# Gate and up projections of a SwiGLU by Strassen's scheme, with the down projection as a phase of its own

## What is computed

```
def rms_norm(x, g):
    y = xf * lax.rsqrt(jnp.mean(xf * xf, axis=-1, keepdims=True) + EPS)
    return (y * g.astype(jnp.float32)).astype(x.dtype)
def swiglu(h, w_gate, w_up, w_down):
    return (jax.nn.silu(h @ w_gate) * (h @ w_up)) @ w_down

x = x + 0.5 * swiglu(rms_norm(x, ff1_norm), ff1_w_gate, ff1_w_up, ff1_w_down)   # 1024 -> 2816 -> 1024
x = x + mixer(rms_norm(x, mix_norm))
x = x + 0.5 * swiglu(rms_norm(x, ff2_norm), ff2_w_gate, ff2_w_up, ff2_w_down)
return rms_norm(x, final_norm)
```

## Time and profile before

| | us |
|---|---|
| three runs | 1892.01, 1892.21, 1893.86 |
| median | 1892.21 |
| span of the profiled execution | 1891.5 |
| TensorE busy in it | 1820.5 |
| VectorE, ScalarE, GpSimd busy | 761.9, 455.6, 431.8 |

### The profile page before, as it was taken

The page is one execution under the profiler, slowest core; times in us unless marked ns, Lnnn a source line. Parts: engine busy times, 40 slices in busy tenths (PEclk is TensorE's granted clock), DMA queues, the critical chain, the costliest instruction groups (busy, mean ns, idle before and its releaser), DMA issues.

```text
span 1891.5 us, 22799 instructions
## 1 busy us (share of the span) xinstructions
PE 1820.5 (96%) x8284; PEld 1493.1 (79%) x8284; DVE 761.9 (40%) x1067; ACT 455.6 (24%) x745; POOL 431.8 (23%) x894
## 2 busy tenths in 40 slices
PE   6899999999999999999798799999999999999998
PEld 5788888888888887788576687888888888888886
DVE  5243243334323434612864545334324333432345
ACT  6211211111111113423447434111121111111113
POOL 2588776750000002400333333000000000000003
PEclk8999999999999999899888899999999999999999
DMA  5311212121121111123922031111111111112102
GB/s 129 85 45 45 78 59 74 55 77 45 33 67 44 44 44 45 62 78 76 120 67 67 12 112 56 56 45 55 33 55 55 44 44 55 44 35 65 44 33 89
DMA packets 166442, 112.33 MB, mean 59 GB/s; under 512 B 32576, under 2 KB 156096, under 8 KB 166144
## 3 DMA queue, kind: packets, MB, share of 16 engines
q1 hardware_dynamic: 165120, 107.35, 20.8%
q0 software_dynamic: 1280, 4.42, 0.6%
HBM read 98.68 MB, written 13.07 MB: 59 GB/s over the span
## 4 chain that ended last, share of the span: by engine, by line
PE 88%; ACT 3%; SPq 3%; DVE 2%; DMA 2%; POOL 1%; issue 1%; DVEq 0%; ACTq 0%; POOLq 0%
PE bank L646 28%; PE bank L647 28%; PE bank L648 28%; POOL ssq L1689 1%; SPq L543 1%; PE bank L882 1%; PE bank L883 1%; DMA Mt<-k_scratch 1%; ACT sco L1234 0%; PE bank L884 0%; DVE htmp L1366 0%; ACT hT_hi L1056 0%; PE bank L841 0%; PE bank L661 0%; SPq L535 0%
## 5 line engine op out<-in xcount | busy, mean ns | idle before, releaser
L646 PE MATMUL bank<-hT_hi,w_lo 128*128 128x512 f32 x1728 | 685.3, 397 | 17.4 <-DVE hT_lo L1379 6.2
L647 PE MATMUL bank<-hT_lo,w_hi 128*128 128x512 f32 x1728 | 679.2, 393 | 0.0
L648 PE MATMUL bank<-hT_hi,w_hi 128*128 128x512 f32 x1728 | 678.9, 393 | 0.0
L646 PEld LDWEIGHTS bank<-hT_hi,w_lo 128*128 128x128 f32 x1728 | 328.7, 190 | 92.1 <-issue 14.7
L1332 DVE TENSOR_TENSOR w_lo<-raw,w_hi 128x1024 fp32r<-128x1024 f32 x157 | 193.0, 1240 | 480.8 <-ACT w_hi L1026 480.8
L647 PEld LDWEIGHTS bank<-hT_lo,w_hi 128*128 128x128 f32 x1728 | 328.9, 190 | 69.9 <-issue 1.9
L648 PEld LDWEIGHTS bank<-hT_hi,w_hi 128*128 128x128 f32 x1728 | 328.4, 190 | 69.4
L1689 POOL TENSOR_TENSOR ssq<-ssq,sqt 128x512 f32<-128x512 f32 x54 | 78.1, 1447 | 1106.5 <-ACT sqt L1040 1102.6
L1416 DVE SCALAR_TENSOR_TENSOR xT<-bank,xT 128x512 f32<-128x512 f32 x352 | 241.0, 690 | 188.0 <-PE bank L648 187.9
L646 PE MATMUL bank<-aT_hi,w_lo 128*128 128x512 f32 x704 | 275.1, 391 | 4.0 <-DVE aT_lo L1409 3.1
L648 PE MATMUL bank<-aT_hi,w_hi 128*128 128x512 f32 x704 | 273.9, 389 | 0.0
(11 more groups left out here) (168 smaller groups left out, 980.2 us busy)
## 6 DMA issues: line engine op xcount, KB each, us to landing
raw<-in_ff_w_gate_dram SPq DMA_DIRECT2D x44, 512.0 KB, 3.7
raw<-in_ff_w_up_dram SPq DMA_DIRECT2D x44, 512.0 KB, 3.7
raw<-in_ff_w_down_dram SPq DMA_DIRECT2D x44, 512.0 KB, 3.3
x_in<-in_x_dram SPq DMA_DIRECT2D x8, 512.0 KB, 6.2
out_dram<-osb SPq DMA_DIRECT2D x8, 512.0 KB, 2.7
raw<-in_w_out_dram SPq DMA_DIRECT2D x26, 128.0 KB, 2.9
raw<-in_w_out_dram SPq DMA_DIRECT2D x13, 256.0 KB, 3.3
raw<-in_w_in_dram SPq DMA_DIRECT2D x6, 512.0 KB, 4.2
```

The lines of the kernel that those rows point to most:

```text
L646: nc.tensor.matmul(o, wl, rh, start=first, stop=False)
L647: nc.tensor.matmul(o, wh, rl, start=False, stop=False)
L648: return nc.tensor.matmul(o, wh, rh, start=False, stop=last)
```

## The change

Gate and up matrices are now cut as 2 x 2 blocks: a pair of column tiles (f = 0, 1) by two halves of the 1024 inputs (kh = 0, 1, four k-tiles each); the activations as kh by token half h. One instance (a pair of column tiles of one matrix, 22 per block) used to be 2 x 2 x 2 = 8 block products of 12 matmuls and is now 7, in the Winograd form of Strassen's scheme: products 0 to 6 accumulate into three banks in the order c, d, c, d, c, b, c (`STEP_BANK`), and between them ACT copies the bank out (`take_snap`), because the next product adds on top. DVE forms the four weight sums of each instance (`weight_sum`), the three sums of results (`gate_c12`, `gate_c22`, `gate_c11`) and the products of gate and up (`up`). The seven activation blocks are made once per feed-forward block (`blocks`): 16 sums over 128 x 512 tiles in place, 24 rounded tiles and 24 rests beside those of product 0 (`block_hi` on ACT; `block_lo` on DVE for odd, `blocks_lo` on POOL for even tiles).

```
+STEP_BANK = "cdcdcbc"
+STEP_FIRST = (0, 1, 5)
+SNAPS = [(0, "c"), (1, "d"), (2, "c"), (4, "c")]
+        def product(n, s):
+            o = bank[inst_bank(n, STEP_BANK[s])]
+            pe.wait_ge(ws_lo_done, N_STEP * n + s + 1)
...
+            elif s == 2:
+                pe.wait_ge(snap_taken, 4 * n + SNAP_C11 + 1)
...
+            for k in range(4):
+                last = mm3(o[:, :], wk(ws_hi[s], k), wk(ws_lo[s], k), b_hi[:, k, :], b_lo[:, k, :],
+                           k == 0 and s in STEP_FIRST, k == 3, True)
```

```
+            sp.wait_ge(product_done, N_STEP * (N_INST * w + N_INST - 1) + (2, 4)[w])
+            sp.wait_ge(x_stored, 32 * (w + 1))
+            for k in range(KD):
+                sp.dma_start(xTs[w + 1][:, k, :], xs_d[:, k, :]).then_inc(x_back[k], 16)
+            store_a(w, N_PAIR - 1)
+            for t in range(2, 2 * N_PAIR):
+                load_down(w, t)
+                load_a(w, t)
```

```
-FIRST = [("G", 0, 0), ("G", 1, 0), ("U", 0, 0), ("G", 0, 1), ("G", 1, 1), ("U", 0, 1), ("U", 1, 0), ("U", 1, 1)]
+        def start(s):
+            if s == 0:
                 x_tiles(1)
                 pe.wait_ge(xt_act, 8)
                 pe.wait_ge(xt_dve, 8)
+                pe.wait_ge(normed_done, KD)
                 norm_spread(N_FF1, 1)
+        instance(0, start)
+        for n in range(1, N_INST):
+            if n == 6:
                 c_tiles()
+            instance(n)
+        for g in range(N_PAIR - 1):
+            down(0, g)
+        down(0, N_PAIR - 1, first_half(N_MIX))
```

On ACT, `blocks` puts the first snapshots between the blocks, and the first of them also waits for block 4's rests, because the snapshots lie where that block was formed:

```
+            for s in (1, 2, 4):
+                for kk in range(4):
+                    block_hi(w, s, kk)
+            take_snap(n, SNAP_C11)
+            for kk in range(4):
+                block_hi(w, 3, kk)
+            take_snap(n, SNAP_D)
...
+            if j == 0:
+                wait_hb(act, w, 4, 3)
```

More of the change, by code:

```diff
@@ new lines, in instance, with down @@
+        def instance(n, between=lambda s: None):
+            for s in range(N_STEP):
+                product(n, s)
+                between(s)
+        def down(w, g, after=lambda n: None):
+            t, i = 2 * g, g % 2
+            pe.wait_ge(w_lo_done, U_DOWN[w] + t + 2)
+            pe.wait_ge(a_lo_done, 2 * N_PAIR * w + t + 2)
+            for n in range(16):
+                d, h = n % KD, n // KD
+                c = 16 * (N_PAIR * w + g) + n
+                if n >= 3 or g:
+                    pe.wait_ge(down_taken, c - 2)
+                elif n == 0:
+                    pe.wait_ge(c11_done, N_INST * (w + 1))
+                for f in range(2):
+                    last = mm3(bank[DOWN_BANK[c % 3]][:, :], wk(wd_hi[i][:, f, :], d), wk(wd_lo[i][:, f, :], d),
+                               aT_hi[w][i][:, f, hs(h)], aT_lo[w][i][:, f, hs(h)], f == 0, f == 1)
+                last.then_inc(down_out, 1)
+                after(n)
@@ L1009, in finish, with between @@
                 out_tile((n - 11) // 2)
-        ffn(1, N_FF2, second_half(N_FF2), finish)
+        def between(s):
+            if s == 0:
+                norm_sum(N_FF2, 1)
+                norm_spread(N_FF2, 1)
+        instance(N_INST, between)
+        for n in range(N_INST + 1, 2 * N_INST):
+            instance(n)
+        for g in range(N_PAIR - 1):
+            down(1, g)
+        down(1, N_PAIR - 1, finish)
         out_tile(3)
@@ new lines, in silu @@
+        def silu(n, f, h):
+            w, j = divmod(n, N_INST)
+            dst = sg[w][:, f, hs(h)]
+            src = dst
+            if (f, h) == (1, 0):
+                act.wait_ge(product_done, N_STEP * (n + 1))
+                src = bank[inst_bank(n, "c")][:, :]
+                if j:
+                    act.wait_ge(a_done, 4 * (N_PAIR * w + j // 2))
+            else:
+                act.wait_ge({(0, 1): c12_done, (1, 1): c22_done, (0, 0): c11_done}[f, h], n + 1)
+            act.activation(dst, src, ACT.Silu).then_inc(silu_done, 1)
@@ new lines, in instance, with ahead @@
+        def instance(n, first=False):
+            w, j = divmod(n, N_INST)
+            gate = n % 2 == 0
+            def ahead(s):
+                if j < N_INST - 1:
+                    weight_hi(n + 1, s)
+                elif s in (4, 6):
+                    down_hi(w, (s - 4) // 2)
+            if not first:
+                take_snap(n, SNAP_C11)
+            ahead(0)
+            if not first:
+                take_snap(n, SNAP_D)
+            ahead(1)
+            if not first:
+                take_snap(n, SNAP_C12)
+            ahead(2)
+            ahead(3)
+            if gate:
+                silu(n, 0, 1)
+            take_snap(n, SNAP_C22)
+            ahead(4)
+            if gate:
+                silu(n, 1, 1)
+            ahead(5)
+            if gate:
+                silu(n, 0, 0)
+                silu(n, 1, 0)
+            ahead(6)
@@ L1113, in x_squares, with ffn @@
+        def ffn(w):
+            for n in range(N_INST * w + 1, N_INST * (w + 1)):
+                if n == 6:
+                    c_out()
+                instance(n)
+            for t in range(2, 2 * N_PAIR):
+                down_hi(w, t)
         def x_squares(h):
@@ L1985, in _ @@
                 take_lo(*at_, tile0=4 * (at_[0] - N_ATT), permuted=at_[0] == N_SSM)
-        norm(N_FF2)
+        for i in range(12):
+            add_square(N_FF2, i)
+        for i in range(12, 16):
+            add_square(N_FF2, i)
+            if i == 13 or i == 15:
+                blocks_lo_tile(1, 0, i - 13)
+        blocks_lo(1, 1, N_STEP)
         norm(N_END)
```

1001 lines of the change are left out of this document (641 added, 360 removed).

## The result

| | us |
|---|---|
| changed kernel, four runs | 1859.03, 1862.43, 1863.04, 1865.02, median 1862.74 |
| kernel before, four runs beside it | median 1893.03 |
| ratio | 0.9838, 95% interval 0.9824 to 0.9852 |
| span of the profiled execution | 1863.3 |

The account below looks back on a forecast made before the run. TensorE was taken to bound the kernel. The terms -119.7 + 30.3 + 38.2 + 10.6 + 3.5 = -37.1 on the span of 1891.5 gave 1854.4, forecast 1855 us; likeliest case 1835 to 1875, 8 in 10 range 1828 to 1888.

Parts of the forecast that it names:

- matmuls removed: All 44 instances: one block product of 12 matmuls fewer each, 528 x 0.2267 = -119.7 us, on TensorE at full clock.
- first start: Start of the first block: instance 0 ends at about 88.5, overhead 70.8 against 40.5, +30.3 us; bounds +18 and +40.
- second start: Start of the second block: the same stretch follows the mixer, overhead 42.5 against 4.3, +38.2 us; bounds +25 and +48.
- two seams: Between products and down, twice: 3.3 us for VectorE's product and rests, 2.0 for low clock, +10.6 us; bounds 6 and 16.
- x comes back: Reload of x, second block: loads for the second down group queue behind it and a store, +3.5 us; bounds 0 and 12.
- the turns of VectorE and GpSimd: Block starts: instructions of both engines run one after the other; without this the first stretch would end some 10 us sooner.
- the first copy behind block 4's rests: First start: ScalarE takes the first snapshot only after the rests of block 4, at 65.7 us; product 2 starts there.
- the last copy behind roundings, table load and Silu: First start: product 6 needs the last snapshot, behind four weight roundings, a table load and a Silu, done at 84.7 us.
- The products in steady state: Instances after the starts: VectorE and ScalarE fit within 19.0 us, some 1.4 us in hand per copy, 0 added.
- No cost: the small loads on GpSimd: Parameter loads moved to GpSimd's queue: from about 78 us, there by 125, needed near 150, so 0 us.
- The rival that was nearest: Parameters come too late: VectorE stops in instance 4, then ScalarE, then TensorE; 1892 us at 37 us late; chance 0.08.
- Snapshots become the bound: ScalarE between products of every instance: gain used up from 2.93 us per hand-over, 1905 us at 3.0; chance 0.12.

Follow-up runs that it names:

- run 8: Changed kernel with product 3 of each instance at 24 matmuls instead of 12, so an instance has 96 again: 1970.73 us, ratio 1.0405.
- run 1: Changed kernel with GpSimd issuing the small parameter loads right behind its two rests of block 0, only the loads of c at the end: 1856.58 us, ratio 0.9801.
- run 2: Changed kernel with the small parameter loads back on SyncE's queue, behind the stores of x and before the third weight load: 1852.07 us, ratio 0.9773.
- run 5: Changed kernel with all rests of activation blocks 1 to 6 made by VectorE, none by GpSimd: 1854.17 us, ratio 0.9791.
- runs 6 and 7: Changed kernel with each snapshot copied two and three times in every instance but the first of a block: 1863.5 and 1864.09 us, ratios 0.9842 and 0.984.
- run 3: Changed kernel with ScalarE taking the last snapshot of each block's first instance right behind its last rounding of block 6: 1838.04 us, ratio 0.9701.
- Run 4: Changed kernel with VectorE making the second pair of rests for the first down group ahead of its last two products: 1866.74 us, ratio 0.9851.
- Run 12: Changed kernel with each snapshot copied four times in every instance but the first of a block: 1897.19 us, ratio 1.0019.
- runs 3 and 11: Run 3 has its own line; run 11: changed kernel with edits of run 2, run 3, Run 4, run 5, ScalarE issuing second down group's loads: 1835.75 us, 0.9704.

## Why the prediction came out as it did

| us | forecast | measured | by |
|---|---|---|---|
| matmuls removed | -119.7 | -119.7 | spacing of 0.2267; run 8 |
| first start | +30.3 | +31.5 | instance 0 ends at 89.7, not 88.5 |
| late weight load in instance 2 | 0 | +11.3 | 8.1 and clock; runs 1 and 2 |
| second start | +38.2 | +39.1 | instance 22 ends at 1200.0: 1200.0 - 1137.6 - 19.0 = 43.4, less 4.3 |
| two seams | +10.6 | +13.3 | waits of 4.87, 3.50 and 0.53, and 1.6 and 2.8 by the low clock |
| x comes back | +3.5 | 0 | no such wait |
| not forecast | | -3.7 | see below |
| sum | -37.1 | -28.2 (spans) | |

**Right.** The starts, which are most of the cost, by their own steps: the turns of VectorE and GpSimd (run 5; the stretch took 35.6 in place of 34.3, with a wait of 1.8 us of VectorE for ScalarE in it that I had not; GpSimd's twelve instructions lasted 1.3 to 1.7 us each, and each lengthened the stretch by less than it lasted), the first copy behind block 4's rests, the last copy behind roundings, table load and Silu. The Trainium skill, "GPSIMD Engine Reference", section 1 (Specifications), says that GpSimd's SBUF interfaces are shared with VectorE, with contention when a VectorE instruction has two inputs in SBUF. The trace agrees: block 4's four sums, two inputs each, took 4.63 us beside GpSimd and 2.50 in run 5 without it. The products in steady state add nothing (runs 6 and 7).

**Wrong: "No cost: the small loads on GpSimd".** I asked when they would be there, and they were, at 122.8 (forecast 125), and VectorE's parameter work found them. What I left out is what they do to others: a 1 MB load beside them takes 32.5 us instead of 5.3. The forecast put this overlap at nothing; it cost 11.3 us. The rival that was nearest had the right transfers and the wrong victim: it let VectorE stop at the parameters, in instance 4, not at a weight tile in instance 2. The trace of before held a warning, since the same loads took SyncE's queue 41 us in the earlier trace rows; I had booked this as issue time of a queue. Why the load of 87.7 lands in 17 us and that of 91.8 in 32 isn't shown beyond that the costliest of the small ones (`par`, `b_raw`) were issued from about 88 on.

Shown is that the small loads on GpSimd's queue beside a large transfer make it late; how they do it is open. Two numbers stand against "small pieces hold the engines". In run 3 next to no data (0.00 MB) moved from 87.7 to 92.7 us, right behind the issue of the weight load, with the engines at 1.8%. And on SyncE's queue the pieces were cheaper: from 24 to 55 us the kernel before moved 0.03 MB of them at 13.4% of the engines, 4.2 us of all 16, where GpSimd's queue had 97.4% of 10.3 us for 0.03 MB. Whether the queue or the large load beside them makes the difference, no run separates.

**Mis-sized.** The seams, +10.6 forecast and 13.3 measured; in the first, VectorE was also late by a wait for the store of an earlier pair. The term for x (+3.5) was put in the wrong place: its mechanism, weights queued behind x and a store, is there (VectorE waits 1.6 to 2.0 us for them), but the wait at the seam covers it. Run 4 took the cover away and it appeared, 2.7 and 3.0 us. Of the -3.7 that no step had, 1.6 is a wait in the kernel before ahead of its last down group which the separate phase no longer has, and 0.7 lies in the mixer and the tail; the rest, some 1.4 us, I can't place. Two slips of the forecast's arithmetic are small: 0.69 + 2 x 1.24 is 3.2 and not 3.3 us at a seam, and the upper bound of the first start counts seven products behind the first snapshot where five follow.

**Luck.** The misses partly cancel: 11.3 for the weight load, 2.7 for the seams and 2.1 for the two starts on one side, 3.5 for x and the 3.7 that no step had on the other. The forecast is nearer than its parts.

**The slower rival.** "Snapshots become the bound" was given 2.72 us as cover and 2.93 as the point from which the gain is gone. Run 12 puts a number on it: at 2.90 us the kernel is at 1.0019 of before. As built, a hand-over takes 0.6 of copy and has over 1.2 in hand.

The best of these kernels, runs 3 and 11, stand at 0.9701 and 0.9704. Edits 3 and 4, 5 and 11 with the small loads left on GpSimd's queue but held back were not run.

## What to carry to other kernels

When loads are moved to another queue, ask not only when they arrive but which large transfer is in flight beside them: many small pieces can cost the DMA engines far more than their bytes, 0.03 MB filled ten us of all 16 here, and the one who waits is whoever asked for a large transfer beside them. When a product is added onto a bank that must first be copied, put the copy ahead of all other work of that engine, above all in the first round. A wait that is removed may have been the cover of another; look at what its engine's queue holds behind it before booking the gain.

## What the runs showed of the hardware

- Taking twelve instructions of 128 x 512 off GpSimd and giving them to VectorE shortened a stretch in which both worked by 4.6 us (35.6 to 31.0).
- The packets of 0.82 MB of small loads on GpSimd's queue took 51% of the 16 DMA engines' time over 40 us, those of 2.57 MB in large transfers 30%. A 1 MB load took 32.5 us beside them, and each of x's two 2 MB stores 35.7 us instead of 10.6. The 128 KB loads of `c` land in 3.1 and 3.7 us once the others are gone (run 1); the 64 KB ones of `b_raw` took 22 to 24 us beside x's store, and 19.1 and 6.2 on SyncE's queue with no large transfer beside them (run 2).
- A chain on ScalarE that is 0.18 us per step too slow (2.90 against 2.72) shows in no list of waits of TensorE: the matmuls at a hand-over start 0.32 and 0.31 us apart instead of 0.23 (1321.42, 1321.74, 1322.05 in run 12), and a row lasts 0.39, so no idle time opens. It shows only in the count of matmuls per window, 107 in place of 112.
